# Sample-token delta rule, cached attention and delta norm as small pieces within the prompt-attention units, in one stage with a PSUM bank of their own

## The chip, the cores and the metric

One core of a Trainium2 chip. The metric is device time in microseconds of one execution, the median of the runs shown. All data is fp32. "hi" and "lo" are the two single-pass halves (fp32r) into which large fp32 products are split; small products are issued as plain fp32, which the profile records as two instructions each, while a transpose is one record.

## The reference, cut to what matters

One layer of a hybrid decoder over 1024 prompt tokens and 8 sample tokens (one per sequence). Each token's features (width 1024) are a convolution group (256), a gated DeltaNet group (384 = 6 heads of 64) and a forgetting-attention group (FoX, 6 heads of 64); then an output projection and a SwiGLU feed-forward of width 2816. The parts that the change touches:

```python
# gated delta rule, per token and head (sample tokens: one step from the stored state)
S = a * (I - b k k^T) S + b k v^T;   o = S^T q / sqrt(64)
y_b = rmsnorm(o, norm_b_g) * silu(z)          # prompt and sample tokens
# FoX attention, prompt: causal within the 1024 tokens; samples: 1024 cached positions and the own one
s = q.k / sqrt(64) + cumsum(logf)[t] - cumsum(logf)[s];   y_c = softmax(s) @ v
```

The cached keys and values of a sample sequence lie in 8 pages of 128 tokens, found through a page table.

## The kernel before, in words

The stages run one after the other: norms, input projection with convolution, the prompt's delta rule (with the cached keys' scores beside it), `samples` (L1587), `fox_prompt` (L1831), `mix_and_feed` (L2159). Each stage is a block in which every engine has its own instruction list, written out by hand and worked off in order; semaphores tie the lists together, and a barrier (L91) stands between stages. `m.proj` holds the projections with channels on partitions, `m.yT` the mixed features in the same layout.

**`samples`** has eight PSUM banks for itself. TensorE turns v of the samples into rows (L1666), spreads the gates' rows over all partitions (L1670), turns the peaks of the cached scores (L1674), and then, for 8 sequences and 6 heads, computes v minus k times state: 48 matmuls that spread a v row (L1683) and 48 that add the state's part (L1686). VectorE scales that (L1797), decays the states and adds (L1800, L1803). TensorE sums the squares of the prompt's delta outputs per head (L1698), forms o = state times q (L1706), and multiplies the cached values of the first two sequences (L165, 16 matmuls of 384 columns). An inverse root follows (ScalarE L259 with a table load; VectorE L265 to L269), its transposes (L1723), and 9 matmuls of 344 columns that spread it (L1731), with two VectorE passes per pair of heads behind them (L1824, L1828). SP loads the 48 states in six DMAs, 16 pages of values, and stores the new states.

**`fox_prompt`** walks 24 units (j, i): 3 pairs of heads, and for each 8 query tiles of 128 tokens, the widest first (i = 7 to 0). The opening is the prefix sums of logf (VectorE L2096, TensorE L1939 and L1940), and the bias rows of the first pair: four fills of a bank with 4 matmuls each (L1964), copied out by VectorE and ScalarE in turn (L2028). A step u then does on TensorE: the scores of unit u+1 (L1950, both heads side by side), the fills of a ring of two PSUM banks with up to four transposes of exponents of unit u each (L1973), and for unit u-1 the spread of its totals (L1996) and the values (L2003). VectorE: the shift of unit u+1 (L2107, scores plus bias and their extreme), even ring copies (L2033), the reciprocal (L2112), the product with the spread (L2118). ScalarE: odd ring copies, exponents (L2059), the spread's copy (L2066). GpSimd adds the causal mask (L1933). The ring also carries the bias rows of the next pair, and the cached values of sequences 2 to 5 in step 12 and 6 and 7 in step 18 (L1980), each followed two steps later by three transposes. A sequence of a group writes its own 32 partitions of the bank. A fill n waits until bank n-2 is copied:

```python
                def fill(n):
                    kind, what = ring[n][0], ring[n][1:]
                    if n >= 2:
                        wait_copied(pe, n - 2)
                    bank = ring_bank(n)
```

The order of the work is thus the order in the lists; there is no planner.

Of the kernel before, what the change touches and what calls it, by code (L numbers as in the profile page):

```python
# [6 lines left out]
F32 = mybir.dt.float32  # L7
# [63 lines left out]

O_VALUES = [O_PROJ, O_TAIL_KV] + [O_PROJ + n * KV_BYTES for n in (0, 1, 2, 3, 0, 1)]
EARLY = 2
# [65 lines left out]
def fox_sample_tensors(nc, m):  # L139
# [13 lines left out]
    m.fs_values = [at(f"fs_values{b}", [P, NPAGE, DW], F32, offset=o) for b, o in enumerate(O_VALUES)]  # L153
    m.logf_in = nc.alloc_semaphore("fs_logf_in")
    m.values_in = [nc.alloc_semaphore(f"fs_values_in{s}") for s in range(4)]


def fox_values(pe, m, bank, sequences, done):


    for b in sequences:

        pe.wait_ge(m.values_in[min(b, EARLY)], 16 * NPAGE * (1 if b < EARLY else NS - EARLY))
        for g in range(NPAGE):
            last = pe.matmul(bank(b)[0:H, 0:DW], m.fs_p[:, b, g], m.fs_values[b][:, g], start=(g == 0),  # L165
                             stop=(g == NPAGE - 1))
        last.then_inc(done, 1)


def turn_fox_rows(pe, m, rows, ps_turned, sequences, done, copied):  # L170

    for n, b in enumerate(sequences):
        pe.wait_ge(copied, n + 1)
        for i in range(PAIRS):
            last = pe.transpose(ps_turned[:, i, b], rows[:, n, i * P:(i + 1) * P], m.ident[0:H, 0:H])
    last.then_inc(done, 1)
# [1410 lines left out]
def samples(nc, m):  # L1587

    with Phase(nc) as ctx:
        off = O_H + KD * T * 4
        at = nc.alloc_sbuf_tensor_at
        keys = at("ds_keys", [P, 3, NS, PAIRS], F32, offset=off + 12288 + 1536 + 64 + 384)
        decay_all = at("ds_decay_all", [P, NS, PAIRS], F32, offset=off + 12288 + 1536 + 64 + 384 + 288)
        state = at("ds_state", [P, NS, PAIRS, HD], F32, offset=off)
        x = at("ds_x", [P, NS, PAIRS, HD], F32, offset=off + 6144)
        v_rows = at("ds_v_rows", [NS, DW], F32, offset=off + 12288)
        ab = at("ds_ab", [NS, 2 * H], F32, offset=off + 13824)  # L1600
        ab_all = at("ds_ab_all", [P, NS, 2 * H], F32, offset=off + 13888)
        small = at("ds_small", [TT, 3, NT * H], F32, offset=off + 14720)
        inv_rows = at("ds_inv_rows", [H, T], F32, offset=off + 15584)

        sq = m.proj[:, T_QB:T_QB + PAIRS]
        off += 15584 + T * 4 + 32

        def put(name, shape):
            nonlocal off
            t = at("fs_" + name, shape, F32, offset=off)  # L1610
            n = 4
            for d in shape[1:]:
                n *= d
            off += (n + 31) // 32 * 32
            return t

        N = NS * H
        s_raw, own_all, p, den = m.fs_s, m.fs_own_all, m.fs_p, m.fs_den
        peak = put("peak", [P, N])
        top = put("top", [N, 1])  # L1620
        top_diag = put("top_diag", [N, N])
        rows = put("rows", [H, EARLY, DW])
        assert off <= O_TAIL_KV, off
        ps = ctx.enter_context(nc.psum_tensor("ds_ps", [P, 8, 512], F32))
        (states_in, decay_done, turned, rows_done, ab_turned, ab_done, keys_scaled, x_ready, x_chain, o_done,
         o_copied, stored, squared, summed, with_eps, rooted, inverted, inv_turned, inv_copied, spread, normed,
         chain) = semaphores(
             nc, ctx, *["ds_" + n for n in (
                 "states_in", "decay_done", "turned", "rows_done", "ab_turned", "ab_done", "keys_scaled", "x_ready",
                 "x_chain", "o_done", "o_copied", "stored", "squared", "summed", "with_eps", "rooted",  # L1630
                 "inverted", "inv_turned", "inv_copied", "spread", "normed", "chain")])
        (peaked, peak_turned, topped, diag_done, top_spread, shifted, exp_done, added, den_spread, den_copied,
         values_done, values_copied, values_turned, fox_chain) = semaphores(
             nc, ctx, *["fs_" + n for n in (
                 "peaked", "peak_turned", "topped", "diag_done", "top_spread", "shifted", "exp_done", "added",
                 "den_spread", "den_copied", "values_done", "values_copied", "values_turned", "chain")])
        flat = lambda t: t.rearrange("p b g h -> p (b g h)")

        ps_fox = ps[:, 7]
        ps_o = ps[:, 7, 0:PAIRS * NS * H].rearrange("p (m b h) -> p m b h", m=PAIRS, b=NS)  # L1640
        half = lambda e: slice(e * HD, (e + 1) * HD)

        seq_banks = lambda e: ps[:, 3 * e:3 * e + 3].rearrange("p b n -> p (b n)").rearrange(
            "p (b m v) -> p b m v", b=NS, m=PAIRS)
        per_head = lambda e, c: ab_all[half(e), :, c + e:c + H:2]
        with nc.Block() as block:
# [1109 lines left out]
```

## Time and profile before

| | us |
|---|---|
| median of 3 runs | 1667.34 (1666.53 to 1669.29) |
| the profiled execution, its time | 1668.22 |
| the profiled execution, its span | 1666.4 |
| TensorE busy over the span | 1576.8 (95%) |
| VectorE, ScalarE, GpSimd busy | 784.0, 412.6, 228.4 |
| mean granted TensorE clock | 0.962 of full speed |

The span runs from the first to the last instruction. PE is TensorE's matmuls and PEld its weight loads, which overlap them; DVE is VectorE, ACT ScalarE, POOL GpSimd, SP the engine that issues most DMAs. A matmul's record lasts until its last result is out, so records of neighbours overlap, and the pace is their busy time divided by their count. PEclk is the granted clock, 1.00 for 2.4 GHz and 0.50 for 1.2 GHz. A row of busy time by stretch gives the stretch and its length in us, then for PE, PEld, DVE, ACT and POOL the busy us with the count of instructions, then PEclk, the busy share of the DMA engines and GB/s. A row of groups by line ends with: busy us, mean ns of one | idle us just before them, and who ended it.

### The profile page before, as it was taken

The page shows a single profiled execution, that of the slowest core. Times are in us where ns is not written, and L with a number is a line of the kernel's source. Part 1 is how long each engine was busy: PE and PEld are TensorE (multiplying, and loading weights), DVE is VectorE, ACT ScalarE, POOL GpSimd, SP SyncE. Part 2 cuts the span into 40 slices and gives each one's busy share as a digit, 9 for nine tenths or more (in the row PEclk, how much of TensorE's full clock was granted, in tenths as well). Part 3 has the DMA queues.
Part 4 walks back from the last instruction along what each step waited for, and adds up shares of the span by engine and source line. Part 5 has one row for each costly group of instructions (what it writes and reads, how often), then busy time and mean ns, then how long its engine had stood idle before and what let it go on. Part 6 is the DMA issues. An engine that isn't in the chain of part 4 may idle for free.

```text
span 1666.4 us, 32885 instructions
## 1 busy us (share of the span) xinstructions
PE 1576.8 (95%) x14052; PEld 1468.1 (88%) x14052; DVE 784.0 (47%) x1409; ACT 412.6 (25%) x710; POOL 228.4 (14%) x263
## 2 busy tenths in 40 slices
PE   7999999989998888898998999999999999999995
PEld 6899998989998646556878999999999999999995
DVE  6359787226665324555653334243342332423426
ACT  5312231222222114445553111111101111111112
POOL 4142000019773001110001000000000000000003
PEclk9999999999999568999998999999999999999998
DMA  6222111212221316025230111101111011011122
GB/s 203 69 42 54 39 40 39 63 52 79 80 82 39 98 19 190 2 77 170 84 102 28 62 39 51 64 26 51 39 52 64 28 49 57 33 64 39 39 102 103
DMA packets 114728, 108.76 MB, mean 65 GB/s; under 512 B 15292, under 2 KB 104839, under 8 KB 114568
## 3 DMA queue, kind: packets, MB, share of 16 engines
q1 hardware_dynamic: 87346, 93.37, 17.8%
q10 hardware_dynamic: 24006, 12.12, 2.7%
q0 software_dynamic: 3232, 1.17, 0.6%
q8 instruction: 111, 1.82, 0.5%
q14 instruction: 33, 0.27, 0.1%
HBM read 94.02 MB, written 12.93 MB: 64 GB/s over the span
## 4 chain that ended last, share of the span: by engine, by line
PE 48%; DVE 3%; ACT 2%; issue 1%; DVEq 0%
PE mf_ps L2604 29%; PE mf_ps L2611 15%; PE mf_ps L2564 3%; PE mf_ps L2592 1%; DVE h_lo L2430 1%; ACT h_hi L2327 1%; PE mf_ps L2632 0%; ACT mo_buf L214 0%; DVE mo_buf L2502 0%; DVE mo_x L2506 0%; ACT mo_buf L2384 0%; DVE ff_scaled L2474 0%; PE mf_ps L2574 0%; DVE ff_w_lo L2437 0%; DVEq L2239 0%
## 5 line engine op out<-in xcount | busy, mean ns | idle before, releaser
L2467 DVE TENSOR_TENSOR ff_acc<-ff_acc,mf_ps 128x344 f32<-128x344 f32 x264 | 135.4, 513 | 185.8 <-PE mf_ps L2611 185.6
L2604 PE MATMUL mf_ps<-h_lo,ff_w_hi 128*128 128x344 f32 x1008 | 213.8, 320 | 0.0
L2604 PE MATMUL mf_ps<-h_hi,ff_w_hi 128*128 128x344 f32 x1008 | 213.6, 320 | 0.0
L2604 PE MATMUL mf_ps<-h_hi,ff_w_lo 128*128 128x344 f32 x1008 | 212.7, 319 | 0.0
L2611 PE MATMUL mf_ps<-ff_h_hi,ff_d_hi 128*128 128x344 f32 x528 | 169.9, 322 | 2.0 <-issue 2.0
L2611 PE MATMUL mf_ps<-ff_h_hi,ff_d_lo 128*128 128x344 f32 x528 | 169.6, 321 | 0.0
L2604 PEld LDWEIGHTS mf_ps<-h_hi,ff_w_lo 128*128 128x128 f32 x1008 | 169.2, 188 | 0.0
L2604 PEld LDWEIGHTS mf_ps<-h_hi,ff_w_hi 128*128 128x128 f32 x1008 | 169.1, 188 | 0.0
L2611 PE MATMUL mf_ps<-ff_h_lo,ff_d_hi 128*128 128x344 f32 x528 | 168.9, 320 | 0.0
L2604 PEld LDWEIGHTS mf_ps<-h_lo,ff_w_hi 128*128 128x128 f32 x1008 | 168.8, 188 | 0.0
L2313 POOL TENSOR_TENSOR ff_x<-ff_x,ff_scaled 128x1024 f32<-128x1024 f32 x7 | 16.4, 2359 | 762.7 <-DVE ff_scaled L2474 762.7
L763 PE MATMUL pc_main<-h_hi,in_whi 128*128 128x344 f32 x528 | 118.3, 333 | 1.6 <-PEq L91 1.6
L763 PE MATMUL pc_main<-h_hi,in_wlo 128*128 128x344 f32 x528 | 113.0, 323 | 0.0
L763 PE MATMUL pc_main<-h_lo,in_whi 128*128 128x344 f32 x528 | 112.8, 322 | 0.0
L2611 PEld LDWEIGHTS mf_ps<-ff_h_hi,ff_d_hi 128*128 128x128 f32 x528 | 100.0, 189 | 2.3 <-issue 2.2
L2611 PEld LDWEIGHTS mf_ps<-ff_h_lo,ff_d_hi 128*128 128x128 f32 x528 | 99.7, 189 | 0.0
L2449 DVE TENSOR_TENSOR ff_hid<-ff_hid,mf_ps 128x1032 f32<-128x1032 f32 x21 | 25.8, 1229 | 157.0 <-PE mf_ps L2604 157.0
L2611 PEld LDWEIGHTS mf_ps<-ff_h_hi,ff_d_lo 128*128 128x128 f32 x528 | 99.7, 189 | 0.0
L2437 DVE TENSOR_TENSOR ff_w_lo<-ff_raw,ff_w_hi 128x1024 fp32r<-128x1024 f32 x44 | 53.7, 1220 | 92.8 <-ACT ff_w_hi L2335 92.8
L763 PEld LDWEIGHTS pc_main<-h_hi,in_whi 128*128 128x128 f32 x528 | 87.4, 190 | 6.2 <-issue 5.0
L763 PEld LDWEIGHTS pc_main<-h_lo,in_whi 128*128 128x128 f32 x528 | 89.7, 190 | 0.0
L763 PEld LDWEIGHTS pc_main<-h_hi,in_wlo 128*128 128x128 f32 x528 | 89.6, 191 | 0.0
(440 smaller groups left out, 2520.0 us busy)
## 6 DMA issues: line engine op xcount, KB each, us to landing
fs_keys<-in_cache_k_dram SPq DMA_DIRECT2D x64, 192.0 KB, 2.7
fs_values<-in_cache_v_dram SPq DMA_DIRECT2D x64, 192.0 KB, 2.6
ff_raw<-in_w_gate_dram SPq DMA_DIRECT2D x22, 512.0 KB, 3.9
ff_raw<-in_w_up_dram SPq DMA_DIRECT2D x22, 512.0 KB, 4.1
ff_d_raw<-in_w_down_dram SPq DMA_DIRECT2D x22, 512.0 KB, 5.6
in_raw<-in_w_in_dram ACTq DMA_DIRECT2D x20, 512.0 KB, 3.9
ld_x<-in_x_prompt_dram SPq DMA_DIRECT2D x8, 512.0 KB, 4.2
mo_o_raw<-in_w_out_dram SPq DMA_DIRECT2D x8, 512.0 KB, 5.1
```

The source lines that it names most:

```text
L763: last = pe.matmul(main[s % 2][:, g, 0:TG], a[s % 2][:, k], c[:, k, group(g)], start=(k == 0 and n == 0), stop=(k == KD - 1 and n == 2))
L2313: pool.tensor_tensor(x1[0:n, c], x1[0:n, c], scaled_rows[c % 8][0:n], ALU.add).then_inc(summed_pool, 1)
L2327: last = act.mul(h2_hi[:, k, tokens(c)], columns(turn_banks(c))[:, k, 0:n], g2(k))
L2430: last = dve.scalar_tensor_tensor(out=h2_lo[:, k, tokens(c)], in0=columns(turn_banks(c))[:, k, 0:n], scalar=g2(k), in1=h2_hi[:, k, tokens( ...
L2437: dve.tensor_tensor(w_lo[t % 2][:], raw[t % 2][:], w_hi[t % 2][:].bitcast(F32), ALU.subtract).then_inc(w_lo_cut, 1)
L2449: dve.tensor_tensor(in_groups, in_groups, ps[:, hidden_banks[1], 0:TG], ALU.mult).then_inc(hidden, 1)
L2467: dve.tensor_tensor(part, part, ps[:, b, 0:TG], ALU.add).then_inc(down_added, 1)
L2564: last = pe.matmul(into[:, part], a, b[:, part], start=(step == 0 and i == 0), stop=(step == KD - 1 and i == 2))
L2592: last = pe.matmul(bank(3 * t + g)[:, 0:TG], a[:, k], b[:, k, group(g)], start=(k == 0 and n == 0), stop=(k == KD - 1 and n == 2))
L2604: last = pe.matmul(bank(t % 2 * 3 + g)[:, 0:TG], a[:, k], b[:, k, group(g)], start=(k == 0 and n == 0), stop=(k == KD - 1 and n == 2))
L2611: last = pe.matmul(bank(b)[:, 0:TG], w[f][:, n * P:(n + 1) * P], h[f][:, group(g)], start=(f == 0 and r == 0), stop=(f == 1 and r == 2))
```

## The change

`samples` and `fox_prompt` are replaced by one stage, `attend`. PSUM: banks 0 to 3 hold scores, 4 and 5 the ring (now transposes and bias only), 6 the output and the spread of the totals (before: two banks in turn), 7 is `side`, the one bank of all sample pieces. Each step has a plan of pieces:

```diff
+        opening = [("v",), ("ab",), ("peak",)]
+        plan[0] = [("top",)]
+        plan[1] = [("dx", 0), ("dx", 1)]
+        plan[2] = [("dx", 2), ("dx", 3), ("den_sum",)]
+        plan[3] = [("den",), ("sums", 0)]
+        plan[5] = [("o",)]
+        plan[6] = [("sums", 1), ("root",)]
+        plan[7] = [("inverse",)]
+        plan[8] = [("inv", 0), ("inv", 1)]
+        plan[9] = [("values", 0), ("inv", 2)]
+        plan[10] = [("rows", 0), ("norm", 0, 0)]
+        plan[11] = [("norm", 0, 1), ("norm", 1, 0)]
+        plan[12] = [("norm", 1, 1), ("norm", 2, 0)]
+        plan[13] = [("norm", 2, 1), ("norm_last",)]
+        plan[18] = [("values", 1)]
+        plan[19] = [("rows", 1)]
+        plan[20] = [("mix",)]
+        BY_ACT = ("v", "ab", "o", "values", "rows")
+        NO_BANK = ("den_sum", "root", "inverse", "mix")
```

TensorE's list for a step; the first piece stands ahead of the transposes, a second behind them:

```diff
+                scores(0)
+                fill_side(opening[0])
...
+                fill_side(opening[1])
+                for n in first_bias:
+                    fill(n)
+                fill_side(opening[2])
+                for u in range(U):
+                    if u + 1 < U:
+                        scores(u + 1)
+                    early, late = plan[u][:1], plan[u][1:]
+                    if u > 0:
+                        for what in early:
+                            fill_side(what)
+                    for n in of_step[u][:1]:
+                        fill(n)
+                    if u >= 1:
+                        spread_total(u - 1)
+                    for n in of_step[u][1:]:
+                        fill(n)
...
+                    for what in late:
+                        fill_side(what)
+                    if u >= 1:
+                        values(u - 1)
```

Every `fill_side` first waits until the piece before it has been read out of the bank, and `values(u)` now waits for ScalarE's copy of the spread, since both share bank 6:

```diff
+                    if place_of[what] > 0:
+                        wait_emptied(pe, items[place_of[what] - 1])
...
+                    elif kind == "dx":
...
+                        for c in range(2):
+                            b = 2 * k + c
+                            into = side[:, c * DW // 2:(c + 1) * DW // 2].rearrange("p (i d) -> p i d", i=PAIRS)
+                            for e in range(2):
+                                pe.matmul(into[half(e)], m.ident[0:NS, b:b + 1].to_broadcast([NS, HD]),
+                                          v_rows[:].rearrange("n (i e d) -> n e i d", i=PAIRS, e=2)[:, e], start=True,
+                                          stop=False, skip_group_check=True)
+                            for i in range(PAIRS):
+                                for e in range(2):
+                                    last = pe.matmul(into[half(e), i], keys[half(e), 0, b, i:i + 1].to_broadcast([HD, HD]),
+                                                     state[half(e), b, i], start=False, stop=True, skip_group_check=True)
```

VectorE and ScalarE do their part of a step's pieces behind all of that step's ring copies (VectorE ahead of the reciprocal and the finish); ScalarE's copy of the spread moves between its two exponents, and it squares one pair of the prompt's delta outputs in each of steps 0 to 2. A dx piece holds two sequences: VectorE scales it, and GpSimd decays the states and adds it. The squares are summed in 27 matmuls over tiles of 128 tokens (before 36 of 86). The inverse root is written as hi and lo rows, so that a norm piece is one single-pass matmul of 512 columns; VectorE multiplies it in and GpSimd multiplies by z. GpSimd makes the masks of unit u+2 in step u. All eight sequences' values are two groups of four, in steps 9 and 18, in the side bank. SP's list:

```diff
+                sp.wait_ge(qkv_copied, 1)
+                for b in range(2):
+                    load_pages(sp, m, m.cache_v, b, sample_values[b], values_in[0])
+                wait_filled(sp, ("sums", 0))
+                load_pages(sp, m, m.cache_v, 2, sample_values[2], values_in[0])
+                sp.wait_ge(dx_used, 4)
...
+                sp.wait_ge(stored, 96)
+                wait_filled(sp, ("o",))
+                load_pages(sp, m, m.cache_v, 3, sample_values[3], values_in[0])
+                wait_filled(sp, ("values", 0))
+                for c in range(GROUP):
+                    load_pages(sp, m, m.cache_v, GROUP + c, sample_values[c], values_in[1])
+                wait_filled(sp, ("values", 1))
+                for k in m.o_first[0:3]:
+                    sp.dma_start(m.o_raw[k][:], m.w_out[0, k * P:(k + 1) * P]).then_inc(m.o_in[k], 16)
```

What is computed stays the same.

## Rows read from the trace of the kernel before

**Rows 1.** The page, part 1: busy time, share of the span, instructions.
```profile
PE 1576.8 (95%) x14052; PEld 1468.1 (88%) x14052; DVE 784.0 (47%) x1409; ACT 412.6 (25%) x710; POOL 228.4 (14%) x263
```
**Rows 2.** Busy time by stretch: samples, their start, opening, steps, steps 1 to 3, delta stage.
```profile
547.50:625.30 77.80, 67.01 (x452) 44.89 (x452) 22.60 (x54) 8.92 (x22) 0.02 (x1) 0.57 0.26 62
547.50:591.10 43.60, 40.20 (x378) 33.57 (x378) 13.33 (x42) 4.51 (x9) 0.00 (x0) 0.50 0.46 110
...
625.30:636.80 11.50, 9.63 (x44) 8.07 (x44) 2.61 (x10) 2.64 (x4) 1.27 (x3) 0.61 0.79 263
636.80:762.20 125.40, 109.09 (x1048) 73.90 (x1046) 68.01 (x191) 61.24 (x161) 20.91 (x46) 1.00 0.23 65
...
643.80:661.10 17.30, 15.83 (x164) 11.69 (x162) 10.07 (x26) 9.59 (x23) 3.20 (x7) 1.00 0.63 176
...
440.00:480.00 40.00, 40.00 (x1266) 38.70 (x1264) 27.89 (x45) 10.04 (x22) 31.68 (x25) 1.00 0.30 82
```
**Rows 3.** Groups by line, fox stage: count, busy us, mean ns, idle before, releaser.
```profile
L1973 PE MATMUL fx_ps<-ident,fx_x 128*128 128x128 f32 x216 | 31.4, 282 | 7.1 <-DVE fx_pt L2033 6.1 <-ACT fx_x L2059 0.6 <-ACT fx_pt L2033 0.5
...
L2033 DVE COPY fx_pt<-fx_ps 128x512 f32<-128x512 f32 (+1 forms) x30 | 20.1, 671 | 2.8 <-PE fx_ps L1973 2.7
...
L2033 ACT COPY fx_pt<-fx_ps 128x512 f32<-128x512 f32 (+1 forms) x30 | 15.4, 514 | 42.1 <-PE fx_ps L1973 42.1
...
L1996 PEld LDWEIGHTS fx_ps<-ident,fx_total 128*64 128x64 f32 x96 | 4.8, 134 | 5.7 <-issue 4.0 <-DVE fx_total L2112 1.0
```
**Rows 4.** Timeline of TensorE, step 2: start, length; idle before in brackets.
```profile
652.88 0.66 PE L1973 MATMUL fx_ps<-ident,fx_x 128*128 128x128 f32 x4 [0.50 <-DVE fx_pt L2033]
```
**Rows 5.** Timeline: the cached values of four, then of two sequences.
```profile
703.23 5.34 PE L1980 MATMUL fx_ps<-fs_values,fs_p 128*6 128x384 f32 x64
...
736.84 5.33 PE L1980 MATMUL fx_ps<-fs_values,fs_p 128*6 128x384 f32 x32
```
**Rows 6.** Timeline of the fox stage's opening.
```profile
625.35 0.06 DVE L2093 MEMSET fx_before<- 128x6 f32 x1 [0.98 <-PEq L91]
...
628.26 6.64 PE L1964 MATMUL fx_ps<-ident,fx_neg_c 128*128 128x128 f32 x32 [0.30 <-ACT fx_neg_c L2053]
...
634.84 1.99 PE L1950 MATMUL fx_ps<-proj 64*128 64x512 f32 x8
...
636.85 1.23 DVE L2107 CUSTOM_DVE_ANT_0 fx_x<-fx_ps,fx_bias 128x1024 f32<-128x1024 f32 x1 [2.38 <-PE fx_ps L1950]
```
**Rows 7.** Groups by line, sample stage.
```profile
L1686 PE MATMUL ds_ps<-ds_state,ds_keys 64*64 64x64 f32 x96 | 11.5, 338 | 0.0
L1683 PE MATMUL ds_ps<-ds_v_rows,ident 8*64 8x64 f32 x96 | 11.4, 336 | 0.0
...
L1698 PE MATMUL ds_ps<-head_ones,proj 128*86 128x2 f32 x66 | 9.8, 286 | 0.0
...
L1706 PE MATMUL ds_ps<-proj,ds_state 64*64 64x1 f32 x96 | 5.3, 242 | 0.0
...
L1670 PE MATMUL ds_ps<-ds_ab,ident 8*128 8x12 f32 x16 | 3.6, 363 | 0.0
```
**Rows 8.** Groups by line, 40 us of the prompt's delta stage, clock 1.00.
```profile
L1453 PE MATMUL dl_ps<-dl_tt,dl_level 64*64 64x64 f32 x240 | 8.3, 218 | 0.0
```
**Rows 9.** The page, part 5: a single-pass matmul of the feed-forward stage.
```profile
L2604 PE MATMUL mf_ps<-h_hi,ff_w_hi 128*128 128x344 f32 x1008 | 213.6, 320 | 0.0
```
**Rows 10.** Groups by line, sample stage: the table load for the root.
```profile
L259 ACT ACT_TABLE_LOAD x1 | 1.3, 1283 | 0.0
```
**Rows 11.** Timeline of the prompt's delta stage, GpSimd and VectorE.
```profile
449.17 1.96 POOL L1279 TENSOR_TENSOR dl_level<-dl_lt,levels 128x384 f32<-128x384 f32 x2
450.40 0.94 DVE L1375 TENSOR_TENSOR dl_kept<-state,dl_exps 128x192 f32<-128x192 f32 x1
...
457.78 0.35 DVE L1375 TENSOR_TENSOR dl_kept<-state,dl_exps 128x192 f32<-128x192 f32 x1
```
**Rows 12.** Timeline: SP issues 32 pages in the fox stage.
```profile
627.35 34.90 SPq L199 DMA_DIRECT2D fs_values<-in_cache_v_dram  x32
```

More of the change, by code:

```diff
@@ new lines, in attend @@
+        v_rows = put("v_rows", [NS, DW])
+        ab = put("ab", [NS, 2 * H])
+        ab_all = put("ab_all", [P, NS, 2, PAIRS])
+        keys = put("keys", [P, 2, NS, PAIRS])
+        qkv = put("qkv", [P, 3 * PAIRS, NS])
+        assert off <= far_values + KV_BYTES, off
+        off = far_values + KV_BYTES
+        peak = put("peak", [P, N])
+        top = put("top", [N, 1])
+        top_diag = put("top_diag", [N, N])
+        small = put("small", [P, 3, (NC + 1) * H])
+        assert off <= O_FOX, off
@@ L1985, in fill, with spread_total @@
                         for i in range(PAIRS):
-                            last = pe.transpose(bank[:, i * P:(i + 1) * P], rows[:, i * P:(i + 1) * P], m.ident[:])
-                    last.then_inc(turned, 1)
-                def values(u):
-                    j, i = units[u]
+                            last = pe.transpose(side[:, i * P:(i + 1) * P], rows[:, i * P:(i + 1) * P], m.ident[:])
+                    last.then_inc(side_filled, 1)
+                def spread_total(u):
                     pe.wait_ge(inv_done, u + 1)
@@ L2033, in empty @@
                     last = copy(pt[u % 2][:, b0:b1].rearrange("p b t -> p (b t)"), bank[:, 0:(b1 - b0) * P])
-                elif kind == "values":
-                    s, = what
-                    eng.wait_ge(rows_set, 1)
-                    if s > 0:
-                        eng.wait_ge(turned, ring.index(("rows", s - 1)) + 1)
-                    for c in range(len(sample_groups[s])):
-                        last = copy(rows[c * 32:c * 32 + H], bank[c * 32:c * 32 + H, 0:DW])
-                else:
-                    s, = what
-                    b0, count = sample_groups[s][0], len(sample_groups[s])
-                    for i in range(PAIRS):
-                        src = bank[:, i * P:(i + 1) * P].rearrange("p (c h) -> p c h", h=32)
-                        last = copy(m.fs_out[:, i, b0:b0 + count], src[:, 0:count, 2 * i:2 * i + 2])
                 last.then_inc(copied[n % 2], 1)
@@ L2068, in _ @@
+                beside(opening[1])
                 for n in first_bias:
@@ new lines, in _ @@
+                dve.memset(before[:, 0], 0.0).then_inc(summed_before, 1)
+                for t in range(1, NC):
+                    dve.wait_ge(summed_before, t)
+                    dve.tensor_tensor(before[:, t], before[:, t - 1], m.gates[:, t - 1, 0:H], ALU.add).then_inc(
+                        summed_before, 1)
+                dve.wait_ge(logf_added, 1)
+                den_step(dve.tensor_reduce(peak[:].rearrange("p (b h) -> p b h", b=NS),
+                                           m.fs_s[:].rearrange("p b g h -> p b h g"), AX_X, ALU.max))
@@ L2138, in _ @@
                     shift(0, e)
+                beside(opening[2])
                 for u in range(U):
@@ L2150, in _ @@
                             empty(dve, dve.tensor_copy, n)
+                    for what in plan[u]:
+                        beside(what)
                     invert(u)
```

618 lines of the change are left out of this document (315 added, 303 removed).

## The prediction, made before the changed kernel was run

> **What bounds the kernel now.** I read the page first: TensorE is busy for 95% of the span [rows 1], so the question is what the change takes off TensorE's path, not off another engine. Then the busy time by stage [rows 2]. The sample stage takes 77.8 us, from its first instruction to the first of the fox stage; TensorE is busy for 67.0 of them, and the other engines together for some 31. TensorE alone therefore sets its length, and its granted clock there is 0.57 of full speed on average, 0.50 (1.2 GHz) over the first 43.6 us. The fox stage has an opening of 11.5 us (clock 0.61) and 24 steps, one per unit, in 125.4 us at clock 1.00 (2.4 GHz), with TensorE busy for 109.1, VectorE for 68.0, ScalarE for 61.2, GpSimd for 20.9. So in the steps too TensorE is the bound, with 16.3 us of gaps; VectorE and ScalarE idle half of the time. Most of the gaps before a transpose group wait for a copy out of the two ring banks [rows 3], 0.50 us in step 2 [rows 4]. The gain must come from two sources: sample work runs at 2.4 instead of 1.2 GHz, and its chains of dependent small steps fall into time in which TensorE has other work.
>
> **Removed.** The whole sample stage: 77.8 us [rows 2]. It ends the path of every engine, so all of it goes. The cached values of two sequences, multiplied in it one after the other, go into the two groups of the fox stage, which grow from 4 and 2 sequences to 4 and 4. A group of four took 5.34 us and one of two 5.33 us [rows 5]: the sequences of a group run side by side in the array, so the larger group is costed at nothing (bounds: 0, and 5.3 us if four were not to fit beside each other, which rows 5 exclude). The barrier between the stages is part of the 77.8.
>
> **Opening, longer.** Before, bias fills (6.64 us) and then the first scores (1.99 us) stood ahead of the first shift at 636.85 [rows 6]. Now the scores come first, at 1.2 GHz, where their 1.99 us may be up to 4; I take 3.7. They cover the 1.5 us in which TensorE waited for the prefix sums after 625.35, and behind the bias fills a copy, a mask and a hand-over remain, about 1.3 us, in place of 2.0. Turning v adds three transposes, 31.4/216 = 0.145 us each [rows 3], doubled at 1.2 GHz: 0.9. Spreading the gates' rows adds 3.6 [rows 7]. Sum 3.7 - 1.5 - 0.7 + 0.9 + 3.6 = **6.0 us** (bounds 2 and 9: clock up early, or nothing covered).
>
> **Pieces in the steps, TensorE's own work at 2.4 GHz.** These ran at 1.2 GHz before, so I halve them.
> - dx, four pieces: 48 matmuls of 64x64 and 16 of 64x192. The old lines took 11.5 and 11.4 us of overlapping busy time for 48 each; together they fill 19.5 us of the stage, 0.20 us each, halved 0.10. The same shape in the delta stage at clock 1.00 took 8.3/120 = 0.069 [rows 8]. So 3.3 to 4.9 us for the first kind; the second three times as wide, 16 x 0.2 to 0.3 = 3.1 to 4.9. Bounds 6.4 and 9.8; I take 9, nearer the rows with the same operands.
> - sums 0 and 1: 54 records instead of 72, at 9.8/66 = 0.149 us, halved 0.074 [rows 7]; the weights are 128 wide instead of 86, so up to 0.11. Bounds 4.0 and 6.0; taken 5.
> - o: 48 matmuls, 5.3 us halved, 2.6.
> - inv: nine transposes at 0.145, 1.3. norm: six single-pass matmuls of 512 columns; 344 columns took at most 213.6/1008 = 0.21 [rows 9], so 0.3 each with the small last one, 2.0. peak, top and den: 0.5.
>
> Sum **20.4 us** (16.8 to 22.2). Each of the 23 pieces is also a hand-over, a semaphore wait in TensorE's queue; the 24 spreads of the totals have 5.7 us of idle weight loading ahead of them [rows 3], 0.24 each, so about 0.2 each is **4.5 us** (2 to 8).
>
> **Waits that the pieces bring.** All share one bank, so a second piece of a step must wait until the first is read out, and the reader stands in its own queue behind that step's ring copies. There are nine such pieces (dx 1, dx 3, sums 0, inv 1, inv 2, norm 0 0, 1 0, 2 0 and the last). After TensorE's last fill VectorE owes a copy, 0.67 us, and the piece's own pass over 384 or 512 columns, about as long: TensorE idles for 0.8 to 1.3 us. inv 1 needs a ScalarE copy and a VectorE subtraction, 1.8; inv 2 waits for four row copies by ScalarE, 2.2. Queued behind TensorE's wait are the values of the unit before and the next scores, and for these wait VectorE's finish and shift. Together 3 x 0.8 + 0.9 + 3 x 1.3 + 1.8 + 2.2 = **11 us** (4 to 20).
>
> **Credits.** A piece put between the scores and the first transposes lets VectorE finish its first shift, so that the ring copy comes sooner; the old wait there totals 7.1 us on TensorE in the steps [rows 3]. Thirteen of the 24 steps have such a piece, and spreading the totals now fills the same gap in all of them. The samples' mix leaves the last steps. I take **-6 us** (-2 to -8). The single output bank makes the values wait for ScalarE's copy of the spread; hidden, since that copy stands ahead of the second exponents, and about 0.5 us in a wide step if not.
>
> **At nothing, with cover.** ScalarE gets some twenty pieces at 0.5 us [rows 3] and two more table loads of 1.3 us [rows 10] against 64 us of idle time in the steps; the loads fall where the wide scores of unit 8 run. Without that cover they cost 2 to 3 us. GpSimd gets 14 passes of 384 or 512 columns, at 1.96/2 = 0.98 us per 384 columns [rows 11], against 104 idle; masks are now made two units ahead. SP's queue: 8 pages take 8.7 us [rows 12]; for the first group the last 8 are issued behind the stored states, between steps 5 and 9, some 20 us; the second group's 32 pages (34.9 us) have steps 9 to 18, over 50 us. The three weight loads move from the fox stage's start to step 18 and land before the end. If late, the wait is added to the step whole.
>
> **A rule weighed.** In the delta stage one VectorE product of 192 columns took 0.94 us while GpSimd was reading, and 0.35 us without it [rows 11]. If each of GpSimd's 14 new passes held VectorE up by those 0.6 us and TensorE with it, the sum would be 8 us larger. The Trainium skill, "SBUF — State Buffer", section "Who interferes with whom", restricts this: a VectorE instruction with two SBUF inputs contends with a reading GpSimd instruction, one with at most one SBUF input does not, outside the two-port modes. By that rule, with which the two rows agree, the pieces here, which read PSUM on one side, lose nothing. The sum leaves the 8 us out and the worse rival holds them.
>
> **The sum.** -77.8 + 6.0 + 20.4 + 4.5 + 11 - 6 = **-41.9 us**. The profiled execution took 1668.22 us with a span of 1666.4; it becomes 1626.3. It stands 0.9 above the median 1667.34, so the forecast is **1625.5 us**.
>
> **Rivals.**
> - *The gaps swallow more (0.12).* Low ends throughout: 3 + 16.8 + 2 + 4 - 8 = 17.8 given back, 1607. For it: 16.3 us of gaps and an idle VectorE. Against: the gaps are short and many.
> - *The shared bank costs more (0.17).* Nine full round trips of 2 us, 23 hand-overs of 0.35, credits of 3: 6 + 20.4 + 8 + 18 - 3 = 49.4, so 1639; with the 8 us of GpSimd contention 1647. For it: in-order queues with three engines per piece.
> - *The clock falls in steps 1 to 3 (0.06).* These steps have 15.8 us of TensorE work [rows 2] and get 14 more, of few rows or few columns. In the old sample stage such matmuls were dense for 43.6 us and the clock stayed at 0.50 [rows 2]. Run at 1.2 GHz they cost 30 more, less some 4 of waits: 1651. Against: the delta stage's 64x64 matmuls ran at 1.00 for 40 us [rows 2, 8], and scores and values stand between the pieces.
> - *Pages late (0.03).* SP waits for the stored states and then for "o"; 8 us lost at step 9: 1633. This is also how the change would not do what it says: the pieces are beside the units, but a unit stands still for them.
> - *Slower (0.02).* The clock never rises in the merged stage. 129 us of work would take twice as long, less the 16 us of gaps: about +113, so 1738. It decides from 42 us of full-clock work run at 1.2 GHz, a third of the stage. Against: the same scores, transposes and values raised the clock before 636.8 and held it for 125 us.
>
> **The numbers.** Forecast case 0.60. The range must hold the first two rivals' values: 1607 to 1647, which leaves out the clock and the slow case and the tails. About 0.2% (3.3 us) is what a measurement of this kernel can tell from no change. Faster 0.97, same 0.01, slower 0.02.
>
> **What would show it.** Right: from the first instruction of the merged stage to the first shift about 17.5 us; clock 1.00 from there to the end; the steps take about 155 us with TensorE busy for 130; TensorE waits before the nine second pieces of 1 to 2 us, put down to VectorE or ScalarE; groups of values still 5.3 us; the feed-forward stages unchanged. Wrong: steps over 175 or under 143 us, clock below 0.9 in any of steps 1 to 9, a wait for a DMA at step 9 or 18, or ring waits that grow instead of shrinking.

## The result, and the profile after

The changed kernel takes 1657.9 us (median of 9 runs, 1653.8 to 1663.1) against 1667.3 (9 runs, 1661.6 to 1672.7): ratio 0.9945, 95% interval 0.9927 to 0.9964. It is faster, by 9 us and not by 42; the forecast of 1625.5 and its range, 1607 to 1647, both miss. The profiled execution took 1657.9 us, with a span of 1656.2. Medians here and below are of fast executions; one of e6, at 3034.8 us, is left out of its median.

Busy time by stretch of the changed kernel: the opening (first scores to second scores), the 24 steps, and the gap to the next stage; then three stretches of the steps between changes of the clock. They answer to [rows 2].

```profile
551.88:567.70 15.82, 11.90 (x64) 9.09 (x64) 6.68 (x17) 3.75 (x12) 3.14 (x7) 0.79 0.61 154
567.70:752.13 184.43, 154.51 (x1378) 102.60 (x1378) 77.08 (x207) 68.88 (x180) 36.46 (x61) 0.89 0.26 74
752.13:757.04 4.91, 0.00 (x0) 0.03 (x1) 2.86 (x5) 3.58 (x4) 0.00 (x0) 0.61 0.50 183
...
603.00:613.30 10.30, 10.30 (x62) 9.95 (x63) 0.48 (x3) 0.00 (x0) 0.00 (x0) 0.50 0.08 20
613.30:633.80 20.50, 18.15 (x230) 13.29 (x230) 9.26 (x30) 10.24 (x26) 3.52 (x8) 1.00 0.62 154
633.80:640.60 6.80, 6.13 (x24) 3.12 (x24) 2.29 (x8) 1.76 (x5) 0.54 (x2) 0.50 0.32 89
```

The same cut of the kernel before, from its second scores to the end of its last values:

```profile
639.29:760.89 121.60, 109.06 (x1046) 73.89 (x1046) 65.34 (x186) 59.93 (x158) 20.46 (x45) 1.00 0.22 64
```

The account, in us of the two profiled executions (the steps run from the second scores to the end of the last values). The sample stage is gone, -77.8. From the first instruction of the attention stage to its second scores it is 15.8 in place of 14.0, +1.8. The steps take 184.4 in place of 121.6, **+62.8**. The stage begins 4.3 later than the sample stage did (551.9 against 547.55; the code ahead of it is the same), and what follows the last values is 1.4 shorter. Sum -10.3, against -10.2 between the spans. So nearly everything that went missing is in the steps, where TensorE is busy for 45.5 us more, idle for 17.4 more, and granted 0.89 of its clock in place of 1.00.

TensorE's waits in the steps and just ahead of them (engine, what it writes and line, what it waited for: total us, times, longest):

```profile
PE at_ps L1925 <- ACT at_spread L1992: 11.1, 11, 2.8
PE at_ps L1791 <- DVE at_neg_max L2094: 4.1, 3, 3.7
PE at_ps L1882 <- ACT at_rows L2034: 3.6, 1, 3.6
PE at_ps L1882 <- DVE at_inv_hl L2169: 3.2, 1, 3.2
PE at_ps L1886 <- DVE yT L2175: 2.5, 2, 1.4
PE at_ps L1886 <- ACT fs_out L2041: 2.2, 1, 2.2
PE at_ps L1849 <- DVE at_dx L2143: 1.9, 2, 1.2
PE at_ps L1889 <- DVE yT L2175: 1.4, 1, 1.4
...
PE at_ps L1871 <- DVE fs_den L2152: 0.9, 1, 0.9
```

The first row is the values group of a unit (L1925) waiting for ScalarE's copy of the spread: 11.1 us, where the kernel before has no such wait. Of the second, 3.7 us are the wait for the first shift; it ends where the steps begin, at 567.70, and counts with the opening. The seven others are the second pieces of steps, 15.7 us in 9 waits. The ring waits of [rows 3], 7.1 us, are down to 0.9. TensorE of the kernel before is idle for 12.5 us over the same cut, and these are its two largest rows (of the second, 2.5 us are again the wait for the first shift, ahead of the steps):

```profile
PE fx_ps L1973 <- DVE fx_pt L2033: 6.1, 10, 0.8
PE fx_ps L1950 <- DVE fx_neg_max L2107: 5.0, 3, 2.5
```

The longest spread wait, in ScalarE's timeline (start, length, engine, line, operation):

```profile
631.74 1.28 ACT L1985 ACT_TABLE_LOAD   x1
633.03 1.15 ACT L1985 ACTIVATE at_x<-at_x,at_neg_max 128x1024 f32<-128x1024 f32 x1
634.08 0.19 ACT L1985 ACTIVATION_READ_ACCUMULATOR at_x<-at_x,at_neg_max 128x1 f32 x1
634.18 0.24 ACT L1992 COPY at_spread<-at_ps 128x128 f32<-128x128 f32 x1
```

ScalarE loads a table and takes 1024 columns of exponents of the next unit, then makes the 0.24 us copy for which TensorE has stood since its spread of 631.24.

That leaves the clock. Its record shows eight stretches at 1.2 GHz within the steps, 41.0 us together; before there was none. What TensorE did ahead of each:

| at 1.2 GHz | ahead of it on TensorE |
|---|---|
| 568.9 to 572.3 | the 3.7 us wait for the first shift |
| 592.8 to 596.2 | the 1.2 us wait of dx 3, then its products of 192 and 64 columns, which ended at 592.5 |
| 603.0 to 613.3 | a 0.9 us wait, then 1.6 us of two-column products (sums 0) |
| 633.8 to 640.6 | within the 2.8 us spread wait |
| 647.4 to 650.8 | the 3.2 us wait of inv 1 |
| 661.1 to 667.9 | within the 3.6 us wait of inv 2 |
| 681.6 to 685.0 | the 1.4 us wait of norm 1 0 |
| 705.4 to 708.9 | within the 2.0 us spread wait |

**The theory (W+C)**: the steps lost their time to waits on hand-overs through two shared banks, and again to the clock that fell around those waits. **Rivals**: L, the clock falls for the pieces' narrow products, not for the waits; H, the spread wait only took idle time that was there anyway; D, pieces that come later are late for their readers.

### The profile page after: what moved, and what is told of

Read it like the earlier page. It is cut to its first block, busy times and chain, and to the rows that moved or that the text cites. A ratio compares the mean times of both kernels' runs of the same rounds, so it can differ in the third digit from the quotient of the medians.

```text
span 1656.2 us, 32683 instructions
## 1 busy us (share of the span) xinstructions
PE 1558.7 (94%) x13952; PEld 1453.5 (88%) x13952; DVE 774.1 (47%) x1378; ACT 412.5 (25%) x715; POOL 245.8 (15%) x282
## 4 chain that ended last, share of the span: by engine, by line
PE 48%; DVE 3%; ACT 2%; issue 1%; DVEq 0%
PE mf_ps L2666 29%; PE mf_ps L2673 15%; PE mf_ps L2626 3%; PE mf_ps L2654 1%; DVE h_lo L2492 1%; ACT h_hi L2389 1%; PE mf_ps L2694 1%; ACT mo_buf L188 0%; DVE mo_buf L2564 0%; DVE mo_x L2568 0%; ACT mo_buf L2446 0%; DVE ff_scaled L2536 0%; PE mf_ps L2636 0%; DVE ff_w_lo L2499 0%; DVEq L2301 0%
```

## Experiments

The runs stand on several chips, so versions are best compared by their ratio to the kernel before on the same chip; each comes with its 95% interval.

**e1: the spread copy first.**

```diff
-                        exponents(u + 1, 0)
                         if u >= 1:
                             copy_spread(u - 1)
+                        exponents(u + 1, 0)
```

> Against the changed kernel (1657.9 us). Theory W+C (the steps lost their time to waits of TensorE on hand-overs, and to the clock that fell after those waits): with the spread copy of step u-1 ahead of the first exponent, the values groups' wait for it falls from 11.1 us in 11 waits to under 3, two of the stretches at 1.2 GHz (those that began behind the 2.8 us wait of step 7 and the 2.0 us wait of step 15, 10 us together) go, which gives back up to 5 us more; the exponents come some 0.5 us later in each step, which costs 0 to 3 us: 1643 to 1652 us. Rival L (the clock falls because the pieces have few columns, not because of waits): the wait goes and the low stretches stay, 1648 to 1656. Rival H (the spread wait was hidden behind what the groups needed anyway, as I costed it): 1655 to 1661.

1649.2 us; ratio to before 0.9886 (0.9862 to 0.9909). The steps took 175.5 us, 8.9 less. Its waits:

```profile
PE at_ps L1791 <- DVE at_neg_max L2094: 5.5, 5, 3.7
PE at_ps L1925 <- ACT at_spread L1992: 3.6, 8, 0.8
```

7.5 us of spread waits are gone (3.6 are left where under 3 were expected) and 1.4 came back ahead of scores. The low stretches of 633.8 and 705.4, 10.2 us, are gone with the waits in which they began; the one behind the wait of inv 1 is 6.8 long instead of 3.4, so 34.1 us are left. H falls.

**e2: one banked piece a step.** The plan spread over all 24 steps, no step with two fills of the side bank:

```diff
-        plan[1] = [("dx", 0), ("dx", 1)]
-        plan[2] = [("dx", 2), ("dx", 3), ("den_sum",)]
-        plan[3] = [("den",), ("sums", 0)]
+        plan[1] = [("dx", 0)]
+        plan[2] = [("dx", 1), ("den_sum",)]
+        plan[3] = [("dx", 2)]
+        plan[4] = [("dx", 3)]
+        plan[5] = [("den",)]
+        plan[6] = [("sums", 0)]
...
```

> Against the changed kernel (1657.9 us): never two pieces that fill the side bank in one step. Theory W+C: the second pieces' waits (about 15.7 us in 9) fall to under 4, and of the 41 us at 1.2 GHz within the steps at least half go, worth some 8 to 12 us; the light piece of delta sums (9.0 us at a mean clock of 0.59) may keep its own low stretch: 1632 to 1650 us. Rival L (few-column pieces bring the clock down, waits don't): waits go, the low stretches stay about 40 us: 1645 to 1652. Rival D (later pieces are late for what needs them, the stored states and the page loads wait): the time ends between 1650 and 1665.

1635.4 us; 0.9788 (0.9770 to 0.9806). Steps 166.3 us, 18.1 less. Its waits:

```profile
PE at_ps L1933 <- ACT at_spread L2000: 15.0, 16, 2.0
PE at_ps L1799 <- DVE at_neg_max L2102: 4.1, 3, 3.7
PE at_ps L1890 <- ACT at_rows L2042: 1.2, 1, 1.2
```

Piece waits went from 15.7 us to under 2; 3.9 of that came back as more spread waits, since TensorE now reaches its values sooner and ScalarE doesn't. Low time is 26.3 us: 14.7 less, where at least half of the 41 was expected to go. D is not seen: no wait for a DMA. The profiled execution took 1643.0 us, the slowest of the four against a median of 1635.4, so its steps and low time may be on the high side.

**e3: both cures.**

> Spread copy first and one piece a step. Theory W+C: both kinds of waits and most of the low stretches go, 1622 to 1640 us, and the gain over the changed kernel is more than the sum of the waits taken away (about 20 us). Rival L: 1636 to 1646, with 30 us or more still at 1.2 GHz in the steps. Rival D: no better than the spread copy alone.

1622.9 us; 0.9720 (0.9689 to 0.9751). Steps:

```profile
564.96:716.74 151.78, 140.62 (x1378) 93.64 (x1378) 75.45 (x207) 68.71 (x180) 36.41 (x61) 0.95 0.31 89
```

32.6 us less than in the changed kernel and 30.2 more than before the change. The prediction gave the steps 29.9 us more (20.4 + 4.5 + 11 - 6). Low time 14.3 us. That the two sums meet is luck: e3's 30.2 are 24.4 of work, 7.2 of clock and 1.3 less idle time than before the change, by the account further on, where the prediction had 24.9 of work, no clock and 5 of idle time.

**e4: work in the waits, which themselves stay.** Ahead of eight second pieces and two values groups:

```diff
+                def warm(what, u):
+                    count = warm_up.get(what, 0)
+                    if count:
+                        n = of_step[u][-1] - 1
+                        wait_copied(pe, n)
+                        for _ in range(count):
+                            pe.matmul(ring_bank(n), m.ident[:], m.proj[:, T_KC, 0:512], start=True, stop=True)
```

> The changed kernel with 18 idle-time fp32 products of a 512-column tile (0.85 us each at full clock by the shift of the same shape; into a bank of the ring that is free) put on TensorE where it waits for a copy; the waits themselves stay. Theory W+C: the engine isn't idle ahead of the groups, so of the 41 us at 1.2 GHz in the steps 15 us or more go, which is worth 7 us or more; the products that are longer than the waits cost 2 to 5: 1648 to 1656 us. Rival L, or a clock that falls by chance: the low stretches stay near 41 us and the products are added, 1657 to 1668.

1642.3 us; 0.9837 (0.9819 to 0.9855), faster than expected. Steps:

```profile
565.05:735.56 170.51, 157.65 (x1414) 99.97 (x1414) 76.99 (x207) 68.81 (x180) 36.41 (x61) 0.97 0.27 76
```

The useless work itself:

```profile
L1917 PE MATMUL at_ps<-proj,ident 128*128 128x512 f32 x36 | 17.8, 613 | 0.7 <-ACT at_pt L1990 0.4 <-DVE at_pt L1990 0.2
```

A kernel that does 36 records more of useless work is 13.9 us faster in its steps. Low time costs half its length (shown below), so the 13.9 come out as 18.5 of useless work, 17.0 less idle time (12.9 against 29.9) and 15.4 less for the clock. 10.2 us of low time are left in two stretches: one behind the wait for the first shift, which was not filled, and one over the two-column products of sums 0, though a useless product had filled the wait ahead of them. That is the plainest evidence for the clock's part, and that the waits drew it down; but L keeps the sums.

**e7: two of the pairs put back into e3** (inv 0 with inv 1, values 0 with inv 2).

> The version with both cures (1622.9 us), with two of the nine pairs put back: inv 0 with inv 1, and values 0 with inv 2, whose second pieces waited 3.2 and 3.6 us in the changed kernel. Theory W+C: both waits come back (about 6.8 us of idle TensorE) and behind each a stretch at 1.2 GHz of 3.4 to 6.9 us, which costs another 2 to 6: steps 8 to 13 us longer, 1631 to 1636. Rival L: the waits alone, no new low stretch, 1628 to 1630. Rival H (the idle time was there anyway, spread over the steps): 1622 to 1626.

1630.9 us; 0.9798 (0.9775 to 0.9821). Its two waits, and the stretches around them:

```profile
PE at_ps L1888 <- DVE at_inv_hl L2175: 3.2, 1, 3.2
PE at_ps L1888 <- ACT at_rows L2040: 3.1, 1, 3.1
```

```profile
639.20:643.38 4.18, 1.03 (x9) 0.72 (x10) 2.42 (x5) 2.83 (x7) 0.47 (x2) 1.00 0.01 2
643.38:646.90 3.52, 3.52 (x30) 2.98 (x32) 0.84 (x2) 0.57 (x1) 0.00 (x0) 0.52 0.00 0
...
658.00:664.92 6.92, 3.84 (x41) 2.23 (x33) 1.16 (x3) 4.32 (x11) 0.46 (x1) 0.93 0.35 95
664.92:674.20 9.28, 9.28 (x57) 7.19 (x59) 2.84 (x10) 1.68 (x7) 0.91 (x2) 0.50 0.64 185
```

Both waits come back, and the clock is at 0.50 behind each (third number from the end). Steps 163.4 us, 11.6 longer than in e3, more than the 6.3 of the waits. The time, 7 to 8 us above e3's and e10's, lies between the two forecasts and does not decide between them, only against H (the intervals of e7 and of e3 and e10 lie apart); the clock record does, with 3.4 and 10.2 us at 1.2 GHz that begin at the two waits and that e3 and e10 don't have at these places. Against e10, the same code as e3 in a later run, whose last 12.5 us of steps ran at 1.2 GHz, the steps are only 6.4 longer.

**e5: sums 0 in three parts.** 16 products in each of steps 5, 6 and 7, no copy between. The first part is now a second piece of its step, behind den, and norm 0 1 stands with norm 0 0 in step 16, so two pairs come back with the split.

> Against the version with both cures (1622.9 us, its steps 151.8 us with 14.3 us at 1.2 GHz, of which 6.8 lie over the delta sums): the 48 products of two columns are issued as 16 in each of three steps, no copy between them, and the pieces behind them move on. Theory P (a piece of few columns brings the clock down when it is long enough to stand alone): the low stretch over the sums goes, their 48 products take some 5 us in place of 9, and the steps end 3 to 5 us earlier: 1617 to 1621. Rival (that stretch fell by chance or for the wait ahead of it): the sums stay near 9 us or a low stretch comes elsewhere, 1621 to 1625.

1632.9 us; 0.9795 (0.9779 to 0.9811): a miss, 9 to 12 us slower than the version with both cures by the ratios. The three parts took 2.0, 3.6 and 2.0 us with the clock at 0.50 from 611.7 to 621.9, and again from 632.2 to 635.6. Both forecasts had it no slower than 1625. Its steps are 160.5 us, 3.4 more than e10's, with as much low time (29.5 against 29.6) and 3.3 us more idle, of which 1.8 are the waits of the two pairs and 1.2 a wait for a page of values. Splitting saved no low time, but the run doesn't test the split alone.

**e6: the same, with the gates' broadcast (ab) behind the first bias fills** on TensorE and ScalarE, and the keys behind the first masks on GpSimd.

> The same as the split sums, with the broadcast of the gates (16 products, 2.0 us) moved from ahead of the first bias fills to behind them, where TensorE waits 3.7 us for the first shift. Theory O (the opening is a chain of bias fills, copies, masks and the first shift): the second scores start 1.5 to 2 us earlier after the first ones, the wait ahead of them shrinks from 3.7 to under 2, and the low stretch that begins in it may go too: 2 to 4 us faster than the split sums. Rival: the keys on GpSimd come later and hold the masks or the first delta piece, so 0 to +1 us.

1626.4 us; 0.9762 (0.9746 to 0.9778), more than the 2 to 4 us forecast. The opening took 12.6 us against 18.2, the wait in it 1.1 against 3.7, and the steps 161.1 against 160.5. But of the opening's 5.6 us the clock has a share: 12.6 us of it stood at 1.2 GHz in e5 and 5.1 in e6, and half of the difference is 3.8.

**e10, e8, e9**, three on one chip: e3 once more as yardstick; sums 0 and o in the wide steps 8 and 9; e3 with the later ab.

> The version with both cures once more, on the chip of the runs beside it, as their yardstick: 0.972 of the kernel before (1619 to 1627 us), with 10 to 20 us at 1.2 GHz in its steps.

> The version with both cures, with the two light pieces (delta sums, 48 products of two columns; delta outputs, 96 of one column) out of the narrow steps 6 and 7 and in the wide steps 8 and 9, and the pieces behind them arranged around that; two pairs of norm pieces stand in wide steps, about 1 us of wait each. Theory D (few-column products on top of a narrow step make the stretch light, and the clock falls there): no low stretch between steps 5 and 9, the low time in the steps falls by the 6.8 us of that stretch, worth 3.4, against 2 us of new waits: 1619 to 1624, 0 to 3 us faster than its yardstick. Rival P (the piece alone brings the clock down wherever it stands): a low stretch of 6.8 us over the sums in step 8, and 1 to 3 us slower than the yardstick. Rival Q (where it falls is chance): low time the same, elsewhere.

> Both cures, and the broadcast of the gates behind the first bias fills instead of ahead of them (no split of the sums). The opening as a chain of bias fills, copies, masks and first shift gets 1.9 us shorter, and the wait of 3.7 us ahead of the second scores shrinks to about 1: 2 to 5 us faster than its yardstick, 1616 to 1622. Rival (the opening's 5.6 us in the split version were the clock's, which stood at 1.2 GHz in one opening and not in the other): within 1.5 us of the yardstick.

e10: 1624.0 us, 0.9741 (0.9726 to 0.9756). e8: 1631.6, 0.9774 (0.9757 to 0.9791). e9: 1621.8, 0.9723 (0.9699 to 0.9747). In e8 a low stretch of 10.2 us (618.7 to 628.9) lies over sums 0 in the widest step too, and values 0, closer behind o than in e3, waited 2.2 us with no releaser in the profile: theory D of that run fell, and the stretch that its rival P named is there; but e8's 7 us over its yardstick are not P's 1 to 3. Its steps are 3.7 longer than e10's with 5.7 us less low time, so by idle time alone (14.9 against 9.9), and its opening took 18.3 against 15.7, 12.8 us of it at 1.2 GHz against 6.6. e9 is 2 us below e10 with overlapping intervals, so neither its forecast nor its rival is decided; its opening is 12.6 us against 15.7, and 3.2 us less of it at 1.2 GHz make 1.6 of that. The two profiles of one code, e3 and e10, have 14.3 and 29.6 us of low time in the steps (10 to 20 were expected of e10), so part of where the clock falls isn't set by the code. And e10's 29.6 are what rival L of e3 had asked for: with both cures a single profile can still be at 1.2 GHz for that long, 10.2 us of it from within sums 0.

**e11: the same 48 products over 65 columns in place of 2**, on top of e3. They also run tile by tile instead of pair by pair, and wait for all three squares first.

```diff
-                            for i in range(PAIRS):
-                                pe.wait_ge(squared, i + 1)
-                                for c in range(NC):
-                                    last = pe.matmul(side[:, c * H + 2 * i:c * H + 2 * i + 2], sq[:, i, c * P:(c + 1) * P],
-                                                     m.head_ones[:, 0:P:HD], start=True, stop=True)
+                            pe.wait_ge(squared, PAIRS)
+                            for c in range(NC):
+                                for i in range(PAIRS):
+                                    at = c * H + 2 * i
+                                    last = pe.matmul(side[:, at:at + HD + 1], sq[:, i, c * P:(c + 1) * P],
+                                                     m.head_ones[:, HD - 1:P], start=True, stop=True)
```

> The version with both cures (its yardstick: 1624.0 us, 0.974 of the kernel before), with the same 48 products of the delta sums, each over 65 columns in place of 2: column by column in rising order, so that each product's surplus is overwritten by the next, and the results are the same. In every version so far a stretch of 6.8 to 10.3 us at 1.2 GHz began within these products or just behind them, in a narrow step, split over three, or in a wide step. Theory P (few columns, not the wait and not the step they stand in): the products take 6 to 7 us (weights of 128x128 bound them, 0.124 us each before), and that stretch goes or shrinks to 3.4: 2 to 5 us faster than the yardstick, 1618 to 1622. Rival (what counts is that weights are loaded for little work, at 65 columns as at 2; or the clock falls there by chance): the stretch stays, 1623 to 1628.

**e12: e11 with the later ab.**

> The same with the gates' broadcast behind the bias fills (1621.8 us without the wide sums): if theory P holds, 1615 to 1620, the fastest of all; by the rival 1620 to 1625.

e11: 1621.7 us, 0.9734 (0.9706 to 0.9762), no different from e10 by these intervals. e12: 1613.0, 0.9692 (0.9662 to 0.9722), the fastest of all and 2 us under its forecast: 54 us under the kernel before, and 42 under the changed one by the ratios. The sums of e10, then those of e11 and of e12:

```profile
600.64 8.73 PE L1879 MATMUL at_ps<-head_ones,at_sq 128*128 128x2 f32 x48
```

```profile
608.02 5.57 PE L1880 MATMUL at_ps<-head_ones,at_sq 128*128 128x65 f32 x48
```

```profile
600.95 5.57 PE L1880 MATMUL at_ps<-head_ones,at_sq 128*128 128x65 f32 x48
```

Over 32 times as many columns the 48 records are 3.2 us shorter than in e10, because the clock stays up over them; against e3, where it fell only in their last microsecond, they are 0.4 shorter (5.94). Low time in the steps is 10.2 us in e11 and 8.6 in e12. Both still have a stretch at 1.2 GHz further on, within the 96 one-column products of o (e11, 6.8 us) or 1.8 us behind them (e12, 3.4 us); e11's is as long as the one that began in e3's sums. So L was half right: the clock fell within the two-column products, or between their parts in e5 and e6, in all eleven profiles that have them, in e9 and e10 with no wait ahead of them, and in neither profile with the same products 65 columns wide. What that is worth in time is not shown. It is not the whole of it, as e4 and e7 show.

**One account for all.** If low time costs half its length, TensorE's busy time less half its low time must be the same work in every version with the same products:

| | steps | busy | low | busy - low/2 | idle |
|---|---|---|---|---|---|
| before | 121.6 | 109.1 | 0 | 109.1 | 12.5 |
| changed | 184.4 | 154.5 | 41.0 | 134.0 | 29.9 |
| e1 | 175.5 | 151.0 | 34.1 | 134.0 | 24.5 |
| e2 | 166.3 | 146.5 | 26.3 | 133.4 | 19.8 |
| e3 | 151.8 | 140.6 | 14.3 | 133.5 | 11.2 |
| e7 | 163.4 | 148.3 | 30.7 | 133.0 | 15.1 |
| e8 | 160.7 | 145.7 | 23.9 | 133.8 | 14.9 |
| e10 | 157.0 | 147.1 | 29.6 | 132.3 | 9.9 |
| e12 | 149.7 | 139.0 | 8.6 | 134.7 | 10.7 |

It is, to within some 1 us either way (e5 132.5, e6 134.3, e9 133.2, e11 134.0). If low time is counted only where TensorE was busy in it, the twelve profiles lie between 133.3 and 134.8. The Trainium skill, "TensorE: Matmul & The Clock Gate", section "HAM oscillation — how this bites in real kernels", reckons the cost of 53.3 us of throttled time as half of it, 26.7; the column that stays level agrees. So the +62.8 us of the steps are **24.9 of work, 20.5 of clock and 17.4 of idle time**.

## Why the prediction was wrong, by its own steps

- *Removed, -77.8*: right, and the two values groups of four take 10.7 us together (e12), as those of four and two did.
- *Opening, +6.0*: +1.8, just under its lower bound of 2. To the first shift it was 13.4 us in place of the 17.5 foretold. The clock was up from 555.3 to 558.7, so ab took 1.95 us and not 3.6, and the bias fills 5.46 and not 6.64. But the opening had 3.7 us of waiting for the first shift that I did not see could hold ab; e6, e9 and e12 put it there.
- *Pieces' own work and hand-overs, 20.4 + 4.5 = 24.9*: right in sum, since busy time less half the low time grew by 24.9. The pieces' share can be read from e12, where the clock was up over nearly all of them. By line their records add up to 25.2 us:

```profile
L1880 PE MATMUL at_ps<-head_ones,at_sq 128*128 128x65 f32 x48 | 5.6, 276 | 0.0
L1862 PE MATMUL at_ps<-at_state,at_keys 64*64 64x64 f32 x96 | 4.5, 226 | 0.0
L1857 PE MATMUL at_ps<-at_v_rows,ident 8*64 8x192 f32 x32 | 4.3, 346 | 0.0
L1895 PE MATMUL at_ps<-at_inv_hl,head_hl 44*128 44x512 f32 x6 | 3.8, 633 | 0.0
L1872 PE MATMUL at_ps<-at_qkv,at_state 64*64 64x1 f32 x96 | 3.0, 193 | 0.0
L1891 PE MATMUL at_ps<-ident,at_small 128*6 128x128 f32 x9 | 1.5, 272 | 1.2 <-ACT at_rows L2043 1.2
```

  But records of neighbours overlap, and only 18.7 us of e12's steps are covered by pieces alone. A norm piece shows it. In e12's timeline its record begins while the scores ahead of it still run:

```profile
574.39 1.35 PE L1799 MATMUL at_ps<-proj 64*128 64x512 f32 x8
575.67 0.54 PE L1857 MATMUL at_ps<-at_v_rows,ident 8*64 8x192 f32 x4
...
676.60 1.35 PE L1799 MATMUL at_ps<-proj 64*128 64x512 f32 x8
677.71 0.48 PE L1895 MATMUL at_ps<-at_inv_hl,head_hl 44*128 44x512 f32 x1
678.11 0.66 PE L1822 MATMUL at_ps<-ident,at_x 128*128 128x128 f32 x4
```

  From the start of the scores to the start of what follows it is 1.28 us without and 1.51 with a norm piece, so the piece costs 0.23 where I had 0.3. Taken so, from start to start, the four dx are 7.7 us (I took 9), sums 6.1 (5, upper bound 6), o 2.9 (2.6), inv 1.0 (1.3), norm some 1.7 (2.0): about 20 in all. The other 5 us are no idle time at semaphores, as I had costed them. About 2.4 lie at the spreads of the totals, which take 0.37 us from start to start among the transposes (e12) where they took 0.27 ahead of the values (before), 24 times; the rest has no place that the traces show. That 4.5 was so near is luck.
- *Second pieces, 11*: 15.7, within its bounds. inv 1 took 3.2 where I had 1.8, inv 2 3.6 for 2.2, norm 0 0 2.2 for about 1: in all three ScalarE reads the bank, and the step's second exponents (0.84 to 1.06 us) stand ahead of that in its queue. I had counted the reader's own work and one copy.
- *Credits, -6*: right; the ring waits fell by 6.2.
- *"The single output bank makes the values wait for ScalarE's copy of the spread; hidden"*: **the first step that failed**. 11.1 us. I put the copy ahead of the second exponents and left out that it stands behind the first, 1.15 us on a wide unit, and behind a table load of 1.3 us, which I had costed at nothing as well. With the copy ahead of the first exponents 3.6 us were left (e1). The kernel before, with two such banks in turn, has no such wait.
- *The clock at 1.00 in the steps*: **the step that failed most**. 20.5 us. I had it as a rival of 0.06, tied to steps 1 to 3 and the narrow products of dx. The dx products all ran at full clock. It fell around second pieces' waits and the wait for the first shift, most of which my own sum contained, around two spread waits, and within sums 0 (10.3 of the 41.0 us). I priced every wait by its length alone.
- *Pages and GpSimd*: right. No wait for a page in the changed kernel. All six of VectorE's norm passes took 0.74 to 0.75 us, the two of 681.59 and 689.69 too, during which GpSimd was at work throughout, so the 8 us were rightly left out. The second of the two rows they were weighed by was misread, though: at 457.78 GpSimd was at work as well (L1279 to 457.92, then L1267), and the product took 0.35 all the same. Four later ones of its line, from 527.80 to 542.36, had no GpSimd instruction beside them and took 0.35 too, so a product of 0.94 did lose 0.6, but not each one beside GpSimd does.
- *The text's own signs of being wrong*, "steps over 175", "clock below 0.9 in any of steps 1 to 9", both came. The rival of the shared bank wasn't it: its 1639 and 1647 are waits again, without their second price. The clock's rival has a time nearer to the measured one, 1651, but for another reason: 30 us of work at 1.2 GHz in steps 1 to 3, for the narrow products of dx.

The steps' difference adds up. Forecast +29.9, measured +62.8: 20.5 for the clock, 11.1 for the spread waits and 4.7 for longer waits of second pieces, less 3.4 for other waits, which shrank by more than I had given them.

With both cures the version lies at 1623 to 1624 us, near the forecast, though not by the forecast's terms (see e3): the gain was there, and the change as made gave three quarters of it back.

The 4.3 us by which the stage began late are the clock's too: of what lies ahead, 23.9 us ran at 1.2 GHz against 15.8 in the kernel before, and half of the difference is 4.1. The code there is the same in all versions, so why it differs stays open; the stage's first scores came between 544.7 and 552.4 us, later by and large where more of what lies ahead ran at 1.2 GHz (10.5 us in e10, 29.6 in e2).

## What to carry to other kernels

When a stage of small pieces is folded into one that keeps TensorE busy, price each new wait twice: its length, and the half of whatever TensorE then does at 1.2 GHz. Not every wait had that second price here, but seven of the eight stretches began around one. Products of one or two columns in a row can have it without a wait. Price the work from start to start, not by the length of records. A bank shared by two uses is only as fast as the engine that empties it, so look at what that engine has ahead of the copy in its queue, and give a shared bank at most one piece per step. If a wait can't go, work put into it can be worth more than it costs (e4), though taking the waits away was worth twice as much (e3).

## What the runs showed that I had not expected

- Useless products in the waits made the steps 13.9 us shorter (e4), and a wider form of the same 48 products was faster than the narrow one, 5.57 against 8.73 us (e11 against e10).
- The clock fell around waits as short as 1.2 us, but not at each: in the changed kernel none at the 2.2 us wait of norm 0 0 (ended at 672.7) nor at the 1.4 us wait of the last norm piece (695.7), in e2 none at one of 2.0 us (ended at 647.0). What decides between them stays open, as does why e3 and e10 differ by 15 us of low time.
- Which part of e12's lead over e9 (8.8 us, 5 by the ratios, with overlapping intervals) is the wide sums is not settled; e11 over e10 gave 2.3, also within the intervals.
